# A fused two-block transformer kernel: the normalised memory's high and low parts start 64 bytes off the weights' alignment

## What is computed

```
def memory_cross_attention(hn, mem, w_xq, w_xkv, g_mem, g_xq, g_xk, w_xo):
    q = rmsnorm((hn @ w_xq).reshape(B, T, 4, 256), g_xq)
    kv = rmsnorm(mem, g_mem) @ w_xkv          # mem is (256, 1024), w_xkv is (1024, 2048)
    k, v = jnp.split(kv, 2, axis=-1)
    k = rmsnorm(k.reshape(B, M, 4, 256), g_xk)
    p = softmax(q k / 16);  return (p v) @ w_xo
```

## Time and profile before

| | |
|---|---|
| median of 3 runs | 1394.93 us (1392.48 to 1395.28) |
| the profiled execution, its own time | 1396.76 us |
| its span, first to last instruction | 1395.0 us |
| TensorE busy (matmuls) | 1360.5 us of the span |
| weight loads busy | 1093.3 us |
| VectorE, ScalarE, GpSimd busy | 661.6, 620.2, 613.6 us |
| mean granted TensorE clock | 0.993 |

### The profile page before, as it was taken

The page is one execution under the profiler, slowest core; times in us unless marked ns, Lnnn a source line. Parts: engine busy times, 40 slices in busy tenths (PEclk is TensorE's granted clock), DMA queues, the critical chain, the costliest instruction groups (busy, mean ns, idle before and its releaser), DMA issues.

```text
span 1395.0 us, 17281 instructions
## 1 busy us (share of the span) xinstructions
PE 1360.5 (98%) x6530; PEld 1093.3 (78%) x6530; DVE 661.6 (47%) x976; ACT 620.2 (44%) x862; POOL 613.6 (44%) x448
## 2 busy tenths in 40 slices
PE   9999999999999999999999999988999999999999
PEld 7877955888876888888888887854878888888887
DVE  5434948355433444344343316588255455554111
ACT  5555228553344443434442123688245545554211
POOL 3444320474430456555564544312336555555453
PEclk9999999999999999999999999999999999999999
DMA  7223211152220243343446433200312222323422
GB/s 268 91 90 110 71 56 66 61 182 91 91 91 1 91 151 136 135 163 138 150 136 258 180 136 106 91 31 31 122 61 90 90 94 91 116 90 136 178 94 91
DMA packets 29215, 155.23 MB, mean 111 GB/s; under 512 B 3056, under 2 KB 4464, under 8 KB 14960
## 3 DMA queue, kind: packets, MB, share of 16 engines
q1 hardware_dynamic: 29168, 154.57, 31.2%
HBM read 152.46 MB, written 2.10 MB: 111 GB/s over the span
## 4 chain that ended last, share of the span: by engine, by line
issue 39%; PE 30%; POOL 26%; DVE 4%; DMA 1%; POOLq 0%; SPq 0%; ACT 0%
POOL wlo L386 26%; PE lin L1367 10%; PE lin L1368 10%; PE lin L1369 10%; DVE small L1024 1%; DVE expd L1035 1%; DMA raw<-w_slabs 1%; PE lin L1578 0%; DVE win L1244 0%; DVE small L1028 0%; POOLq L395 0%; DVE xl L903 0%; DVE xl L879 0%; PE att L1432 0%; PE att L1438 0%
## 5 line engine op out<-in xcount | busy, mean ns | idle before, releaser
L386 POOL TENSOR_TENSOR wlo<-raw,whi 128x512 fp32r<-128x512 f32 x444 | 613.4, 1413 | 766.0 <-ACT whi L413 505.4
L1367 PE MATMUL lin<-xh,whi 128*128 128x512 f32 x1072 | 420.8, 393 | 4.2 <-POOL wlo L386 3.6
L1369 PE MATMUL lin<-xh,wlo 128*128 128x512 f32 x1072 | 417.3, 389 | 0.0
L1368 PE MATMUL lin<-xl,whi 128*128 128x512 f32 x1072 | 417.2, 389 | 0.0
L1367 PEld LDWEIGHTS lin<-xh,whi 128*128 128x128 f32 x1072 | 201.2, 188 | 53.6 <-issue 7.7
L413 ACT ACTIVATE whi<-raw 128x2048 fp32r<-128x2048 f32 x66 | 126.7, 1919 | 261.7 <-PE lin L1369 256.3
L1369 PEld LDWEIGHTS lin<-xh,wlo 128*128 128x128 f32 x1072 | 201.2, 188 | 42.5
L1368 PEld LDWEIGHTS lin<-xl,whi 128*128 128x128 f32 x1072 | 201.3, 188 | 41.4 <-issue 0.5
L1367 PE MATMUL lin<-fh,whi 128*128 128x512 f32 x352 | 137.0, 389 | 0.0
L1369 PE MATMUL lin<-fh,wlo 128*128 128x512 f32 x352 | 136.9, 389 | 0.0
L1368 PE MATMUL lin<-fl,whi 128*128 128x512 f32 x352 | 136.9, 389 | 0.0
(11 more groups left out here) (320 smaller groups left out, 1924.0 us busy)
## 6 DMA issues: line engine op xcount, KB each, us to landing
raw<-w_slabs SPq DMA_DIRECT2D x111, 1024.0 KB, 4.7
adar<-ada SPq DMA_DIRECT2D x48, 512.0 KB, 5.5
decay<-decay SPq DMA_DIRECT2D x4, 512.0 KB, 8.3
h<-x_t SPq DMA_DIRECT2D x3, 512.0 KB, 6.3
out_t<-h SPq DMA_DIRECT2D x3, 512.0 KB, 8.1
rope<-rope SPq DMA_DIRECT2D x2, 512.0 KB, 7.1
memx<-mem_t SPq DMA_DIRECT2D x1, 1024.0 KB, 5.9
adar<-c_row SPq DMA_DIRECT2D x2, 512.0 KB, 6.1
```

Of the source, the lines that this page charges most:

```text
L386: return nc.gpsimd.tensor_tensor(wlo[s][:, ks, :], raw[s][:, ks, :], f(whi[s][:, ks, :]), ALU.subtract)
L1367: nc.tensor.matmul(out, whi_, xhi_, start=first, stop=False)
L1368: nc.tensor.matmul(out, whi_, xlo_, start=False, stop=False)
L1369: return nc.tensor.matmul(out, wlo_, xhi_, start=False, stop=last)
```

## The change

The region begins 128 bytes later and the allocation grows by the same 128 bytes, so everything in the region and behind it moves up by 128 bytes. `memh` and `meml` are then put 64 bytes below their old places in the region: `meml` begins in the 128 bytes that became free ahead of the region, and `memh` takes the last 64 bytes of what was `meml`'s 8 KB. Both begin at 64 modulo 128; everything else of the region stays at 0 modulo 128, and goes from 128 to 256 modulo 512. No instruction is added, removed or reordered.

```
-        region = at[0]
-        at[0] += 88 * 1024
+        region = at[0] + P
+        at[0] += 88 * 1024 + P
         tail = at[0]
...
         memx = rg_sb("memx", [P, KT, M], 16)
-        memh = rg_sb("memh", [P, KT, M], 8, F32R)
-        meml = rg_sb("meml", [P, KT, M], 0, F32R)
+        memh = rg_sb("memh", [P, KT, M], 8 - 1 / 16, F32R)
+        meml = rg_sb("meml", [P, KT, M], -1 / 16, F32R)
```

## The result

The changed kernel takes 1401.29 us in the median (1400.95 to 1404.11, 6 runs) against 1395.39 us of the kernel before in the same runs. The ratio is 1.005, 95% interval [1.004, 1.006]: slower by 0.5%, where no change was forecast, and above the forecast range of 1391.5 to 1398.5 us. The profiled execution has a span of 1399.3 us, 4.3 us more than before.

What follows compares the result with a forecast made beforehand. TensorE, busy 1360.5 of 1395.0 us with a stream of matmuls, was taken as the bound, through the distance between starts. All four terms were 0, sum 0, giving a median of 1394.9 us, range 1391.5 to 1398.5.

Steps and rivals of the forecast that it cites:

- Step (c): Region moved 128 bytes against the weights, 1440 matmuls of 512 columns: taken as 0, bounds 19.2 us either way.
- The rival: Region's 128 bytes matter, the memory's 64 do not: up to 19.2 us slower (1414, chance 0.06) or faster (1376, 0.05).
- step (a): 384 matmuls on memh and meml at offset 64: taken as 0, bounds 13.3 ns a matmul either way.
- the walk: Slab-by-slab reading of the memory's stage through its waits: 13.3 ns saved gives 2.7 to 3.0 us, doubled costs 3.0 to 3.3.
- (b): Writes of memh and meml by ScalarE and VectorE, under the forgetting attention: at most 0.3 us would show, taken as 0.
- (d): DMAs into the region (memory, tables, decays) land 128 bytes further on, still in long pieces: 0.
- The clash: The 13.3 ns stall is two reads clashing: offset 64 avoids it (1392.0 us, 0.12) or worsens it (1398.0, 0.13).

## Why the prediction was wrong

**The bound.** TensorE sets the time, and the distance between starts is what an address can touch: right. That each matmul stands 13.3 ns above one column per tick at the full clock and 0 at the half was the right place to look. The forecast of 1394.9 us in a range of 1391.5 to 1398.5 failed at 1401.29, and the way of the change was wrong with it.

**Step (c) failed.** "I take 0" for the region's 128 bytes is the step that made the prediction wrong. The runs put 6.2 ns on each `fh` and 5.4 on each `xah` matmul: 1056 x 6.2 + 384 x 5.4 = 8.6 us, of the 19.2 that were its bound. The region alone reproduces the loss, 1.0052 against 1.005. The time shows less than 8.6 us: 0.7 us came back from the memory's slabs, and in the profiled executions the clock gave back another 3; that the spans differ by only 4.3 us is in part luck with the clock, whose stretches come and go without the change. The rival was named, with 0.06 for this side, and set down as "nothing speaks for it but that it is untested". The argument against it was unsound: weight tiles begin 512 bytes apart at one distance in time, from which follows that 512 is a whole number of periods, and nothing about 128. The same rows that excluded steps of 512 left every smaller one open; step (c) reached 1440 matmuls on the path and step (a) 384 half hidden ones, yet (a) got the longer thought.

**Step (a)** was wrong in kind and its price small. "Where they begin should average out" fell: key slabs fell from 119.8 to 117.8 ns and value slabs from 119.9 to 115.7. It is a partial saving, 2.0 and 4.2 of the 13.3 ns in the mean. Its worth was to be read from the waits, and there the walk held in the main. With the memory's edit alone a key-slab matmul is 4 to 5 ns faster and a value-slab matmul 2. k1's gain went into a pause of 0.30 us ahead of the statistics behind it, and v3's into the wait ahead of "out" (1.61 us against 1.51 with the region 512 bytes later alone). By the walk, k0, k2, k3, v1 and v2 give 0.12 + 0.16 + 0.24 + 0.10 + 0.10 = 0.7 us, where 0.41 were measured. Two terms fell short: k2, beside its stretch at half clock, took 7.16 us against 7.12 and gave nothing, and GpSimd's four instructions on the path from k3's end to v1 took 5.69 us against 5.54.

**Steps (b) and (d)**, 0 each, held as far as the runs show. The region 256 or 512 bytes later and everything 128 bytes later leave the time as it was, and all of these move the region's DMAs and writes. With `memh` and `meml` 64 bytes down the median write of `memh` still takes 530 ns and that of `meml` 479, against 530 and 480 before.

**The rules of the two pages.** By the Trainium skill, "TensorE: Matmul & The Clock Gate", Part 2, the two read ports are independent, and an offset would have nothing to act on. Here it acts: 227 against 233 ns by 128 bytes of distance. By the Trainium skill, "SBUF — State Buffer", Specifications, the on-chip memory has lines of 16 bytes; an offset of 32 bytes, two such lines, costs 6.6 ns, so lines of 16 bytes do not account for it.

**The clash itself** is argued, not shown. Shown are: for 512 columns, a price that depends on the distance of stream and weights modulo 256, not on their places; a price at each of the distances tried, smallest at 0 for 512 columns and largest at 0 for 256 columns. That two reads meet would fit. How the lengths 256 and 512 come to opposite orders stays open, and so does what gives two paces at 256 columns with the same addresses.

## What to carry to other kernels

A move that is "neutral" because it keeps one alignment is not neutral: count every instruction whose addresses shift against its partner's, and price the largest set first. Here float32r matmuls of 512 columns with their weights loaded beside them were fastest, of the distances tried, with stream and weights at the same start modulo 256 bytes, the weights loaded beside the stream included. If spare bytes are needed in front of a region, take a multiple of 256. Rows that vary by 512 bytes show nothing about a shift of 128.

## What the runs showed that was not expected

At 256 columns the order turns round: distance 0 is the slowest (120 ns), and a stream 64 bytes below its weights the fastest (115 to 116 ns); the key slabs (memory streams) at distance 192 and the value slabs (memory stationary) at distance 64 agree in this, 115 to 116 ns each in the mean, made of slabs at 113 to 114 ns and others at 117.8. A shift of 32 bytes costs a 512-column stream as much as 192 do, and 64 bytes a third of it. In this kernel no arrangement that was tried beats the one of before by more than can be measured.
